# Band attention two tiles ahead in a two-block transformer kernel: four probability buffers, bias and first scores made during the input projection, pooling matmuls later

## The reference, cut to what matters

```python
h = rms_norm(x, norm1_g[l]);  y = h @ w_in[l]            # 1280 columns: q 512, k 128, v 128, pooling 512
a = swa_attention(q, k, v, ...)                          # 8 heads of 64, 2 key/value heads
b = pool_mixer(p, pool_w[l], pool_scale[l])              # 4 groups of 128 channels
x = x + jnp.concatenate([a, b], axis=-1) @ w_out[l]

# swa_attention: each chunk of 64 queries sees its own chunk and the two before it
q = rms_norm(q); k = rms_norm(k)
s = einsum(q, k_band) * HEAD_DIM ** -0.5 + band_bias(rel_bias);  s = where(valid, s, -1e30)
m = maximum(max(s), sink);  p = exp(s - m);  p = p / (sum(p) + exp(sink - m));  o = einsum(p, v_band)

# pool_mixer, group g with window w = 2, 4, 8, 16
d = causal_mean(pf, w) - pf;  o = (d @ pool_w[g]) * pool_scale[g]
```

## Time and profile before

| | |
|---|---|
| median of three runs | 3420.15 us |
| the profiled execution: its own time, its span | 3418.35 us, 3416.6 us |
| busy: PE, PEld, DVE, ACT, POOL | 3212.3, 2605.0, 1901.7, 1121.5, 1193.9 us |
| last matmul of unit 9 ends, about | 105.3 us |
| first scale-and-bias step of the attention | 116.8 us |
| first matmul of the output projection | 177.3 us |
| mean granted PE clock of the execution | 0.973 |

### The profile page before, as it was taken

How to read it: one execution, slowest core, us unless ns; L and a number is a source line. 1 busy time by engine, 2 the same in 40 slices (tenths; PEclk the granted TensorE clock), 3 DMA queues, 4 the chain that set the end, 5 groups by cost and what they waited for, 6 DMA issues and landing times.

```text
span 3416.6 us, 43435 instructions
## 1 busy us (share of the span) xinstructions
PE 3212.3 (94%) x15836; PEld 2605.0 (76%) x15836; DVE 1901.7 (56%) x2893; ACT 1121.5 (33%) x1599; POOL 1193.9 (35%) x490
## 2 busy tenths in 40 slices
PE   6699999999999989999999899887799998999999
PEld 4597668888888878888888678543588886898887
DVE  5648885666666525555555662578643335553333
ACT  4332223444444422222222342355332213232121
POOL 3133333333333344444444312200044443434452
PEclk9799999999999999999999999989899999999999
DMA  4123774555545555555555321100032322222222
GB/s 144 37 87 106 271 281 169 186 192 184 198 175 205 183 202 192 196 196 192 194 196 192 122 74 44 62 1 0 31 111 93 103 94 80 99 82 103 93 98 74
DMA packets 191921, 456.33 MB, mean 134 GB/s; under 512 B 11544, under 2 KB 79256, under 8 KB 189208
## 3 DMA queue, kind: packets, MB, share of 16 engines
q1 hardware_dynamic: 86688, 310.57, 26.5%
q10 hardware_dynamic: 105080, 143.66, 12.2%
HBM read 381.31 MB, written 72.88 MB: 133 GB/s over the span
## 4 chain that ended last, share of the span: by engine, by line
PE 85%; DVE 9%; ACT 3%; issue 1%; DMA 1%; ACTq 0%; SPq 0%; DVEq 0%
PE ps L513 26%; PE ps L514 25%; PE ps L515 25%; PE ps L718 3%; PE ps L686 1%; DVE nb L1744 1%; DVE stats L1763 1%; DVE Ed L1789 1%; PE ps L893 1%; DVE nrm L1445 1%; ACT Ed L1326 1%; DVE Ed L1788 1%; DMA araw<-ada_units 1%; PE ps L695 1%; DVE std L1424 1%
## 5 line engine op out<-in xcount | busy, mean ns | idle before, releaser
L485 POOL TENSOR_TENSOR unit_lo<-unit_raw,unit_hi 128x1024 fp32r<-128x1024 f32 x486 | 1193.7, 2463 | 2196.1 <-ACT unit_hi L985 2195.2
L513 PE MATMUL ps<-hn_hi,unit_hi 128*128 128x512 f32 (+1 forms) x2344 | 923.2, 394 | 33.1 <-DVE hn_lo L1439 15.7
L514 PE MATMUL ps<-hn_lo,unit_hi 128*128 128x512 f32 (+1 forms) x2344 | 898.8, 383 | 0.0
L515 PE MATMUL ps<-hn_hi,unit_lo 128*128 128x512 f32 (+1 forms) x2344 | 897.9, 383 | 0.0
L985 ACT ACTIVATE unit_hi<-unit_raw 128x1024 fp32r<-128x1024 f32 x486 | 505.6, 1054 | 564.8 <-DMA unit_raw<-w_units 495.0
L513 PEld LDWEIGHTS ps<-hn_hi,unit_hi 128*128 128x128 f32 x2344 | 444.4, 190 | 163.1 <-issue 46.7
L515 PEld LDWEIGHTS ps<-hn_hi,unit_lo 128*128 128x128 f32 x2344 | 444.3, 190 | 86.0
L514 PEld LDWEIGHTS ps<-hn_lo,unit_hi 128*128 128x128 f32 x2344 | 445.0, 190 | 81.9 <-issue 3.8
L513 PE MATMUL ps<-gp_hi,unit_hi 128*128 128x512 f32 x1024 | 399.7, 390 | 8.7 <-DVE gp_lo L1702 8.7
L514 PE MATMUL ps<-gp_lo,unit_hi 128*128 128x512 f32 x1024 | 399.6, 390 | 0.0
L515 PE MATMUL ps<-gp_hi,unit_lo 128*128 128x512 f32 x1024 | 399.4, 390 | 0.0
(11 more groups left out here) (249 smaller groups left out, 3969.8 us busy)
## 6 DMA issues: line engine op xcount, KB each, us to landing
unit_raw<-w_units SPq DMA_DIRECT2D x486, 512.0 KB, 3.5
araw<-ada_units SPq DMA_DIRECT2D x96, 512.0 KB, 5.9
act_dram<-stage ACTq DMA_DIRECT2D x32, 1024.0 KB, 6.2
gate_dram<-gst ACTq DMA_DIRECT2D x16, 2048.0 KB, 7.8
gbuf<-gate_dram ACTq DMA_DIRECT2D x32, 1024.0 KB, 6.5
abuf<-act_dram ACTq DMA_DIRECT2D x32, 1024.0 KB, 10.1
x<-x_t SPq DMA_DIRECT2D x8, 256.0 KB, 5.9
x_dram<-x ACTq DMA_DIRECT2D x1, 2048.0 KB, 6.3
```

The costliest lines, as they stand in the source:

```text
L485: nc.gpsimd.tensor_tensor(lo[:, u % RING], raw[:, u % RING], hi[:, u % RING].bitcast(F32), ALU.subtract).then_inc(lo_ready, 1)
L513: mm(dst, wh, ah, start=start, stop=False)
L514: mm(dst, wh, al, start=False, stop=False)
L515: return mm(dst, wl, ah, start=False, stop=stop)
```

## The change

There are four buffers E instead of two (the bias and E[0] move to the `stage` area, which is not in use yet). The load of the bias is issued by ACT at n = 3 instead of n = 9; DVE clears E[0] and adds the mask before the moving means. The scores of tile 0 go into banks 4 to 7, before unit 9; those of tiles 1 to 3 stay in banks 0 to 3. PE keeps the scores two tiles ahead. The pooling matmuls go behind the product with v of tile 1, into banks 0 to 3. The division is made by eight instructions, one for a head, in place of one. The core of the diff, hunks in order of the engines:

```diff
-        E = [at("swa_e0", R0, [P, HEADS, BAND]), at("swa_e1", R0 + 24 * KB, [P, HEADS, BAND])]
+        E = [at(f"swa_e{t}", off, [P, HEADS, BAND])
+             for t, off in enumerate((72 * KB, R0, R0 + 24 * KB, R0 + 16 * KB))]
-        bias = at("swa_bias", R0 + 16 * KB, [P, HEADS, BAND])
+        bias = at("swa_bias", 64 * KB, [P, HEADS, BAND])
+        def band_bank(t):
+            four = ps[:, 0:4, :] if t else ps[:, 4:8, :]
...
# PE
+            def band_scores(t):
+                if t == 0:
+                    pe.wait_ge(qn_done, 5)
+                    pe.wait_ge(rel_copied, 1)
+                elif t == 1:
+                    pe.wait_ge(win_ev, 10)
+                else:
+                    pe.wait_ge(swa_read, t)
+                S, k0 = band_bank(t), P if t == 0 else 0
...
                 else:
+                    band_scores(0)
                     unit_in(u)
...
-            for g in range(4):
-                pe.wait_ge(pool_d, g + 1)
-                mm(ps[:, 4 + g, :], poolw[:, g, :], pT[:, g, :], start=True, stop=True).then_inc(pool_mm, 1)
-            band_scores(0)
+            band_scores(1)
             for t in range(TT):
-                if t + 1 < TT:
-                    band_scores(t + 1)
+                if t + 2 < TT:
+                    band_scores(t + 2)
                 pe.wait_ge(swa_p, t + 1)
                 if t:
                     pe.wait_ge(swa_lo, t)
...
                 last.then_inc(swa_o, 1)
+                if t == 1:
+                    pe.wait_ge(swa_read, TT)
+                    for g in range(4):
+                        pe.wait_ge(pool_d, g + 1)
+                        mm(ps[:, g, :], poolw[:, g, :], pT[:, g, :], start=True, stop=True).then_inc(pool_mm, 1)
+            pe.wait_ge(pool_done, 4)
             pe.wait_ge(swa_lo, TT)
             seam_projection(1, U_WOUT, 0)
# ACT
-                if n == 9:
+                if n == 3:
                     act.wait_ge(rel_stored, 16)
                     act.dma_start(bias[:, :, :], rel_dram[...]).then_inc(bias_in, 16)
                 split_hi(U_WIN + n + AHEAD)
...
+            band_exps(0)
+            band_exps(1)
+            for t in range(2):
+                band_copy(t)
+                band_high(t)
+                band_exps(t + 2)
+            band_copy(2)
+            for g in range(3):
+                pool_high(g)
+            band_high(2)
+            pool_high(3)
+            band_copy(3)
+            band_high(3)
# DVE
+            V.memset(E[0][:, :, 0:P], LOW)
+            dve.wait_ge(bias_in, 16)
+            dve.wait_ge(con2_in, 32)
+            link(V.tensor_tensor(bias[:, :, :], bias[:, :, :], <band mask>, ALU.add))
             for g, w in enumerate(POOL_WINDOWS):
...
+            def band_share(t):
+                e, sm = E[t], swm[t]
                 dve.wait_ge(swa_e, t + 1)
                 link(V.tensor_tensor(sm[:, 6, :], sm[:, 4, :], sm[:, 5, :], ALU.add))
                 link(V.reciprocal(sm[:, 7, :], sm[:, 6, :]))
-                V.tensor_tensor(e[:, :, :], e[:, :, :], sm[:, 7, :].unsqueeze(2).broadcast_to([P, HEADS, BAND]),
-                                ALU.mult).then_inc(swa_p, 1)
+                for h in range(HEADS):
+                    last = V.tensor_scalar(e[:, h, :], e[:, h, :], sm[:, 7, h:h + 1], None, ALU.mult)
+                last.then_inc(swa_p, 1)
...
+            band_max(0)
+            dve.wait_ge(unit_used, U_WIN + 10)
+            band_max(1)
+            band_share(0)
+            for t in range(2):
+                band_max(t + 2)
+                band_share(t + 1)
+                band_low(t)
+            band_share(3)
+            for g in range(3):
+                pool_low(g)
+            band_low(2)
+            pool_low(3)
+            band_low(3)
```

More of the change, by code:

```diff
@@ L153, in build_program @@
         nrm = at("nrm", NT + 8 * KB, [P, 2, T])
-        E = [at("swa_e0", R0, [P, HEADS, BAND]), at("swa_e1", R0 + 24 * KB, [P, HEADS, BAND])]
+        E = [at(f"swa_e{t}", off, [P, HEADS, BAND])
+             for t, off in enumerate((72 * KB, R0, R0 + 24 * KB, R0 + 16 * KB))]
         PTs = at("swa_pt", R0 + 8 * KB, [P, 2 * HEADS, P])
-        bias = at("swa_bias", R0 + 16 * KB, [P, HEADS, BAND])
-        swm = [at(f"swa_small{b}", R2 + 27 * KB + 256 * b, [P, 8, HEADS]) for b in range(2)]
+        bias = at("swa_bias", 64 * KB, [P, HEADS, BAND])
+        swm = [at(f"swa_small{t}", R2 + 27 * KB + 256 * t, [P, 8, HEADS]) for t in range(TT)]
         ptmp = at("pool_tmp", R1 + 16 * KB, [P, 3, T])
@@ L262, in build_program @@
         HALVES = (slice(0, T // 2), slice(T // 2, T))
+        def band_bank(t):
+            four = ps[:, 0:4, :] if t else ps[:, 4:8, :]
+            return four.rearrange("p b n -> p (b n)").rearrange("p (h k) -> p h k", h=HEADS)
         def seam_bank(k, j):
@@ L588, in _ @@
                 .then_inc(rel_mm, 1)
+            def band_scores(t):
[7 more added lines that the diff above has]
+                S, k0 = band_bank(t), P if t == 0 else 0
+                for c in range(HEADS // 2):
+                    for b in range(2):
+                        rows = slice(64 * b, 64 * b + 64)
+                        last = mm(S[:, 4 * b + c, k0:BAND], qT[rows, c, t * P:(t + 1) * P],
+                                  kT[rows, (t - 1) * P + k0:(t + 1) * P], start=True, stop=True)
+                last.then_inc(swa_s, 1)
             for n in range(10):
@@ L609, in _ @@
                         .then_inc(win_bs, 1)
-            pe.wait_ge(qn_done, 5)
-            for g in range(4):
-                pe.wait_ge(pool_d, g + 1)
-                mm(ps[:, 4 + g, :], poolw[:, g, :], pT[:, g, :], start=True, stop=True).then_inc(pool_mm, 1)
-            S = ps[:, 0:4, :].rearrange("p b n -> p (b n)").rearrange("p (h k) -> p h k", h=HEADS)
-            PTp = ps[:, 4:8, :].rearrange("p b n -> p (b n)").rearrange("p (s k) -> p s k", k=P)
[L620 to L630, removed]
-            band_scores(0)
+            PTp = ps[:, 4:8, :].rearrange("p b n -> p (b n)").rearrange("p (s k) -> p s k", k=P)
+            band_scores(1)
             for t in range(TT):
-                if t + 1 < TT:
-                    band_scores(t + 1)
+                if t + 2 < TT:
+                    band_scores(t + 2)
                 pe.wait_ge(swa_p, t + 1)
@@ L638, in _ @@
                     pe.wait_ge(swa_lo, t)
-                else:
-                    pe.wait_ge(pool_done, 4)
                 for s in range(2 * HEADS):
-                    last = nc.tensor.transpose(PTp[:, s, :], E[t % 2][:, s // 2, (s % 2) * P:(s % 2 + 1) * P], ident)
+                    last = nc.tensor.transpose(PTp[:, s, :], E[t][:, s // 2, (s % 2) * P:(s % 2 + 1) * P], ident)
                 last.then_inc(swa_t, 1)
@@ L1105, in _, with pool_high @@
                 split_hi(U_WIN + n + AHEAD)
-            for g in range(4):
+            def pool_high(g):
                 act.wait_ge(pool_mm, g + 1)
-                activation(mix_hi[:, 4 + g], ps[:, 4 + g, :], ACT.Identity,
+                activation(mix_hi[:, 4 + g], ps[:, g, :], ACT.Identity,
                            scale=pc("pool_scale", g, 1)).then_inc(pool_hi, 1)
             def band_exps(t):
-                e, sm = E[t % 2], swm[t % 2]
+                e, sm = E[t], swm[t]
                 act.wait_ge(swa_m, t + 1)
@@ L1117, in band_exps, with band_copy @@
                 activation(sm[:, 5, :], sm[:, 3, :], ACT.Exp).then_inc(swa_e, 1)
-            band_exps(0)
-            for t in range(TT):
+            def band_copy(t):
                 act.wait_ge(swa_t, t + 1)
@@ L1125, in _, with band_high @@
                            ACT.Copy).then_inc(swa_pt, 1)
-                if t + 1 < TT:
-                    band_exps(t + 1)
+            def band_high(t):
                 act.wait_ge(swa_o, t + 1)
@@ L1531, in _ @@
                                        ALU.mult).then_inc(qn_done, 1)
+            o2, w2 = CON2["band"]
+            V.memset(E[0][:, :, 0:P], LOW)
+            dve.wait_ge(bias_in, 16)
+            dve.wait_ge(con2_in, 32)
+            link(V.tensor_tensor(bias[:, :, :], bias[:, :, :],
+                                 con2[:, o2:o2 + w2].unsqueeze(1).broadcast_to([P, HEADS, BAND]), ALU.add))
             for g, w in enumerate(POOL_WINDOWS):
@@ L1546, in _ @@
                                        ALU.subtract).then_inc(pool_d, 1)
[L1548 to L1554, removed]
             def band_max(t):
                 k0 = P if t == 0 else 0
[L1557 to L1561, removed]
+                e, sm, S = E[t], swm[t], band_bank(t)
                 dve.wait_ge(swa_s, t + 1)
@@ L1581, in _, with band_low @@
                 link(V.reciprocal(sm[:, 7, :], sm[:, 6, :]))
-                V.tensor_tensor(e[:, :, :], e[:, :, :], sm[:, 7, :].unsqueeze(2).broadcast_to([P, HEADS, BAND]),
-                                ALU.mult).then_inc(swa_p, 1)
-                if t + 1 < TT:
-                    band_max(t + 1)
```

(10 more changed lines are left out.)

## The result

| | before | after |
|---|---|---|
| median, range, runs | 3420.52 us (3419.89 to 3426.46, 4) | 3398.61 us (3396.07 to 3400.25, 4) |
| ratio of after to before | | 0.9934, 95% interval 0.9920 to 0.9948 |
| profiled execution: own time, span | 3418.35, 3416.6 us | 3399.45, 3397.7 us |
| scores of tile 0 / first matmul of unit 9 (before) | 94.5 us | 95.6 us |
| first scale-and-bias step | 116.8 us | 108.9 us |

The kernel is faster by 21.9 us in the medians and by 18.9 us between the profiled executions. The forecast was 3397 us. Between the two traces the output projection moves by 20.2 us and the stretch behind it is 1.3 us longer; the difference is made in the first 160 us.

The account below looks back on a forecast made before the run. Bound: a late bias, then a ring over DVE, ACT and PE before the output projection. DVE's start at 107 us, attention to 151.7 plus clock allowance to 155.8, against 177.3: 21.5 us off 3418.35, so 3397; eight in ten 3390 to 3407.

Parts of the forecast that it names:

- The earlier start: Before the attention: bias and mask earlier bring DVE's first scale-and-bias step to 107 us, against 116.8.
- ACT's hold: At n = 3 ACT waits some 9 us, until about 75.3, for the DMA storing the bias row; 0.2 us on PE.
- Rival (b): Before the attention: moving means meet further POOL splits, DVE starts at 112 instead of 107; 3402 us, no separate chance.
- The division: On DVE in the attention: eight pieces of 256 columns take 2.4 us in place of one of 2.29.
- The attention: From first scale-and-bias to output projection: DVE's path, then PE's, 107.0 to 151.7 us at full clock, 155.8 with clock allowance.
- The clock: PE in the attention: no pause above 4 us at full clock; a quarter of the way to half clock, 0.25 x 16.6 us.
- The half-clock case: Attention with PE wholly at half clock: ends at 168.3 us, total 3409; cold PE or an unshortened ring, 0.22.
- the ring as long as before: Attention needs 60.5 us as before from 107, ends at 167.5; 3408.6 us; 0.22 together with cold PE.
- The other side: At n = 3: a store completing past 75.5 us holds k, v's queue and PE, eating the gain; chance 0.02.
- The warm rival: Attention: PE warm throughout, no late DVE; PE and ACT bound at 150 us, total 3390; chance 0.10.
- rival (d): At n = 3: ACT's wait for a late store eats the gain; an end at 108 gives 3426 or so; chance 0.02.
- The rest as a block: Everything behind the output projection's start moves earlier unchanged, by the same 21.5 us.

Follow-up runs that it names:

- bias_n5: The change with the bias load issued at n = 5 instead of n = 3; median 3393.9 us, ratio 0.9921 to the kernel before.
- one_div: The change with the division as one instruction again; median 3399.0 us, ratio 0.9930 to the kernel before.
- warm: The change with seven idle matmuls in PE's first two attention pauses; median 3392.9 us, ratio 0.9921 to the kernel before.
- after_again: The change unaltered, measured a second time; median 3394.5 us, ratio 0.9925 to the kernel before.
- f_one: The change with its front part kept but the attention one tile ahead, pooling behind the product of tile 2; median 3411.4 us, ratio 0.9970 to the kernel before.
- bias_n2: The change with the bias load issued at n = 2 instead of n = 3; median 3403.6 us, ratio 0.9950 to the kernel before.
- best_again: The change with bias load at n = 5, pooling matmuls in the copy waits, idle matmuls in PE's first two pauses, second run; median 3394.3 us, ratio 0.9928.
- late_bias: The change with the bias asked for at n = 9 and the mask behind the moving means, as before; median 3404.3 us, ratio 0.9950.

## Why the prediction was right

The total came out 1.6 us above the forecast, inside the range of 3390 to 3407. The gain forecast was 21.5 us; the medians show 21.9, measured again 26.8, and the projection moved by 20.2. By its steps:

- **The earlier start.** 107 us forecast, 108.9 measured. 1.0 us of this is the execution's own later start (root of n = 3 at 66.76 instead of 65.76 us). Right in parts: ACT's hold until about 75.3 (75.97), its price of 0.2 us on PE (no wait). The bias did not hold DVE. Not foreseen: the hold releases three POOL splits in a row, and the scaling of the last q unit sat behind one (2.91 us instead of 0.75), 2.2 us that no term of the sum held. Rival (b) had named the kind, means and splits moved against each other, but not this place. The means were met by two collisions, as summed (2.69 and 2.37 us). That the hold lies on the path was in the sum as 3.5 us of late k; bias_n5 measured 5.2 us at the clearing and, after one more collision of the means, 3.2 us at the first scale-and-bias.
- **The division.** 2.4 us taken, 2.19 measured, one of 2.29 removed. Single pieces are 0.348 us long and start 0.26 apart, since (2.19 - 0.348) / 7 = 0.263. The rule of the Trainium skill ("VectorE: DVE Perf Modes", The DRAIN you can't avoid), taken as the prediction took it, without the exception that the same section makes (an operation that is not held starts earlier), would have given eight full lengths, by an estimate from the 0.348 us 2.8 us. The trace does not agree with that; its 0.263 us between starts agrees with the exception. one_div shows that the edit as a whole moves nothing: 60.7 us of interval against 60.9.
- **The attention.** 48.8 us forecast from the first step to the projection (107.0 to 155.8), 48.1 measured. The order of the path was as written in its first and last parts, DVE up to the division of tile 0 and PE from the product of tile 1 on, with the pooling on the path. It was wrong between them. The sum stayed on DVE through the maximum of tile 2, the division of tile 1 and the low part of tile 0; the chain of waits goes through the half-clock transposes of tile 0 and ACT's exponentials of tile 2 to the copy of tile 1 at 131.83 us. The transposes of tile 1, the sum's way, had ended at 131.1, so this error of order costs less than 1 us. In warm, with these transposes at full clock, the chain of waits runs as the sum had it.
- **The clock.** I said that at full clock no pause of PE would pass 4 us, and allowed a quarter of the way to half clock, 4.1 us. The pause before the scores of tile 2 was 4.88 us, and they and the transposes of tile 0 ran at half clock. Against the full-clock lengths product 1 is longer by 0.9 us, the pooling by 0.8 and product 2 by 1.5, all on the path; transposes 0 are longer by 1.7, of which 1.1 reach the copy of tile 1 by the comparison with warm. That is 4.3 us in all, an estimate. The sentence on pauses was wrong; the allowance covered it. That it did is in part luck: after_again, the same kernel, has its half-clock lengths partly elsewhere (scores of tile 3 at 3.57 us, product 1 at 1.97) and yet an interval of 60.9 us. The two ends that the quarter was set by, 174.7 and 179.5 us for the order before, are printed without their sums and cannot be followed.
- **The rivals.** The half-clock case (168.3 us) and the ring as long as before (167.5) did not come. f_one is the trace of the latter: 60.2 us, 3411.4. The late start at 112 came only in bias_n2, at 113.4, with the total 3403.6 against 3402 named; E[0] was cleared 2.5 us later than in the change there, and the means met three POOL splits instead of two. The other side, ACT's hold reaching PE, was shown at n = 2 with 6.21 us of PE's time. The warm rival's end at 150 us was reached only by best_again, at 150.1, with three further edits.
- **Slips without weight.** The division in eight adds 28 instructions on DVE, not 24 (2921 against 2893 in the profiles). In rival (d) an end of the store at 108 us gives, by the sum's own terms, 3396.9 + (108 - 75.5) = 3429 us before anything is hidden, not 3428.
- **The rest as a block.** Held to 1.3 us between the two traces, but the same stretch varies by 7 us between traces, so part of the agreement of the totals is luck of this size.

## What to carry to other kernels

A gap in front of a ring of engines and the ring itself are two gains. Sum them apart, test them apart (9.3 and 15.3 us here), and expect a little less together (21.3). When a wait is moved forward to hide a transfer, look at what it stops on its own engine: here PE never waited for the engine that stood still, and yet the norms behind it came 5 us later and the attention's first step 3 us later, which two iterations later would not have cost. A start that is earlier also meets other work: of the 5.2 us that bias_n5 gained at the clearing, two collisions with POOL splits took back 4 before the second scale-and-bias. Work that is moved out of a stretch that waits anyway lands on the path when the stretch no longer waits; taking it off is worth no more than the distance to the next engine behind it (2.2 of 4.45 us here). And profile one kernel twice before reading a difference of 1 us: the change alone gave intervals of 61.5 and 60.9 us and medians 4.1 us apart.

## What the runs showed of the hardware

- Tensor-scalar instructions of 128 x 256 elements with a pointer scalar start 0.263 us apart at a length of 0.348; a broadcast multiplication of the same 2048 columns takes 2.29 us, eight of them 2.19.
- The bias load took 5.8 us to land when issued at 76 us and 8.0 us when issued at 105 us, and 7.0 when issued at 107 us in late_bias, on the same queue and with the same bytes.
- Beside a POOL split three instructions of DVE took some 2 us more than by themselves, for all their different sizes: 2.91 us instead of 0.75 (128 x 512 scaling), 2.37 instead of 0.17 (two-column copy), 2.21 instead of 0.17 (eight columns, bias_n5). The maximum over 128 x 2048 at 110.16 us, beside the split at 109.26, kept its 2.29 us.
- With seven matmuls of idle work PE stayed at full clock up to the transposes of tile 1 (warm: scores 2.00, transposes 1.97 and 1.94 us). From product 1 on, behind a pause of 1.97 us, lengths of 2.87 and 3.55 us came again; other pauses of 1.97 us in the same trace were followed by full-clock lengths (1.09 and 1.97).
- The same kernel profiled twice had its half-clock lengths in partly different places (the change and after_again): product 1 2.85 and 1.97 us, scores of tile 3 2.00 and 3.57, last product 1.97 and 2.43.
